# Four unused strips of SBUF that shift where the operands of the matmuls begin

## What is computed

```
def swiglu(h, w_gu, w_down):
    gu = h @ w_gu
    return (jax.nn.silu(gu[..., :D_FF]) * gu[..., D_FF:]) @ w_down       # D_FF = 2816

def first_block(...):                       # x: tokens, z: context
    for i in range(2):                      # two layers
        x = ffn_sublayer(x, ...); z = ffn_sublayer(z, ...)
        # layer 0: short_conv_mixer(x), short_conv_mixer(z); layer 1: window_attention_mixer(hx, hz)
        x = adaln_out(x, yx, ...)
        x = ffn_sublayer(x, ...)            # and z in layer 0
    return x

def second_block(...):                      # x alone
    proj = rms_norm(x, g_mix) @ w_in        # 13 pieces: queries, keys, values, gates
    merged = sigmoid(gate_a) * (nsa_mixer(...) @ w_up_nsa) + sigmoid(gate_b) * (moba_mixer(...) @ w_up_moba)
    x = x + merged @ w_out
    gate, up = jnp.split(rms_norm(x, g_ffn) @ w_ffn_in, 2, axis=-1)
    x = x + (jax.nn.silu(gate) * up) @ w_ffn_out
    return x + sigmoid(rms_norm(x, g_ple) @ w_ple_gate) * (p @ w_ple_proj)
```

## Time and profile before

| | us |
|---|---|
| three timed runs | 2218.05, 2222.94, 2223.88 |
| median | 2222.94 |
| the profiled execution, whole | 2218.97 |
| its span, first to last instruction | 2217.6 |
| mean granted TensorE clock in it | 0.989 of full speed |
| TensorE busy with matmuls | 2121.8 (96%) |
| TensorE busy with weight loads (beside them) | 1914.7 (86%) |
| VectorE busy | 1525.9 (69%) |
| ScalarE busy | 1045.5 (47%) |
| GpSimd busy | 90.1 (4%) |

### The profile page before, as it was taken

The page is one execution under the profiler, slowest core; times in us unless marked ns, Lnnn a source line. Parts: engine busy times, 40 slices in busy tenths (PEclk is TensorE's granted clock), DMA queues, the critical chain, the costliest instruction groups (busy, mean ns, idle before and its releaser), DMA issues. The chain is left out here.

```text
span 2217.6 us, 35178 instructions
## 1 busy us (share of the span) xinstructions
PE 2121.8 (96%) x14546; PEld 1914.7 (86%) x14546; DVE 1525.9 (69%) x2435; ACT 1045.5 (47%) x1675; POOL 90.1 (4%) x67
## 2 busy tenths in 40 slices
PE   6999999999989999999999999997999899999998
PEld 4988889998889888899988889857999887799998
DVE  3665776777675667767566776785767666777665
ACT  5622224663474222257422235675544544665444
POOL 0000000100100000010000001001000101000000
PEclk9999999999999999999999999999999999999999
DMA  7545555455435455544545544502455552245544
GB/s 307 201 166 194 190 181 176 157 183 197 153 134 185 167 200 192 177 162 154 193 163 206 192 166 163 181 23 96 164 217 185 181 200 87 77 157 179 202 172 151
DMA packets 70015, 378.77 MB, mean 171 GB/s; under 512 B 7392, under 2 KB 12384, under 8 KB 42976
## 3 DMA queue, kind: packets, MB, share of 16 engines
q1 hardware_dynamic: 66960, 369.92, 47.5%
q10 hardware_dynamic: 2896, 6.60, 0.8%
HBM read 375.45 MB, written 1.05 MB: 170 GB/s over the span
## 5 line engine op out<-in xcount | busy, mean ns | idle before, releaser
L549 PE MATMUL ps_g<-h,w_hi 128*128 128x256 f32 (+2 forms) x4288 | 985.2, 324 | 25.6 <-DVE h L1044 7.7
L931 DVE TENSOR_TENSOR w_lo<-w_raw,w_hi 128x1024 fp32r<-128x1024 f32 (+2 forms) x614 | 688.1, 1123 | 388.1 <-ACT w_hi L1521 386.7
L1521 ACT ACTIVATE w_hi<-w_raw 128x1024 fp32r<-128x1024 f32 (+2 forms) x614 | 590.0, 967 | 529.6 <-PE ps_g L549 373.1
L549 PEld LDWEIGHTS ps_g<-h,w_hi 128*128 128x128 f32 x4288 | 717.8, 190 | 97.4 <-issue 15.1
L549 PE MATMUL ps_g<-h,w_lo 128*128 128x256 f32 (+2 forms) x2144 | 690.2, 322 | 0.0
L549 PE MATMUL ps_g<-hid,w_hi 128*128 128x256 f32 (+1 forms) x2368 | 498.8, 308 | 13.4 <-DVE y L1113 8.6
L549 PEld LDWEIGHTS ps_g<-h,w_lo 128*128 128x128 f32 x2144 | 406.4, 190 | 32.9
L549 PEld LDWEIGHTS ps_g<-hid,w_hi 128*128 128x128 f32 x2368 | 385.3, 190 | 38.6 <-DVE w_lo L931 9.8
L549 PE MATMUL ps_g<-hid,w_lo 128*128 128x256 f32 (+1 forms) x1184 | 362.1, 306 | 0.0
L549 PE MATMUL ps_g<-b_h,w_hi 128*128 128x256 f32 x1504 | 274.1, 284 | 10.2 <-DVE b_h L1044 7.2
L549 PEld LDWEIGHTS ps_g<-b_h,w_hi 128*128 128x128 f32 x1504 | 231.5, 190 | 18.0 <-issue 17.2
(11 more groups left out here) (274 smaller groups left out, 1588.8 us busy)
## 6 DMA issues: line engine op xcount, KB each, us to landing
w_raw<-in_gu SPq DMA_DIRECT2D x130, 1024.0 KB, 4.8
mod_raw<-in_w_mod SPq DMA_DIRECT2D x128, 512.0 KB, 3.5
w_raw<-in_conv_cu SPq DMA_DIRECT2D x16, 1024.0 KB, 4.8
w_raw<-in_dn00b SPq DMA_DIRECT2D x16, 768.0 KB, 4.2
w_raw<-in_dn01b SPq DMA_DIRECT2D x16, 768.0 KB, 4.2
w_raw<-in_dn10b SPq DMA_DIRECT2D x16, 768.0 KB, 4.2
w_raw<-in_conv_out SPq DMA_DIRECT2D x8, 1024.0 KB, 4.8
w_raw<-in_w_in_a SPq DMA_DIRECT2D x8, 1024.0 KB, 4.9
```

Of the source, the lines that this page charges most:

```text
L549: mm = pe.matmul(at, w[wp][:, k, m * P:(m + 1) * P], acts[ap][:, k, cs], start=(k == 0 and n == 0 and not (one_bank and m)), stop=(k == kc ...
L931: dve.tensor_tensor(w_lo[u % 2][:, cols], w_raw[u % 2][:, cols], w_hi[u % 2][:, cols].bitcast(F32), ALU.subtract).then_inc(lo_made, 1)
L1521: act.activation(w_hi[u % 2][:, cols], w_raw[u % 2][:, cols], ACT.Copy).then_inc(hi_made, 1)
```

## The change

Four tiles that nothing reads or writes are put among the others, and the tile `skip2`, also unused, is made 512 bytes smaller. No instruction is added, taken away or moved, on any engine.

```diff
     b1 = ExitStack()
+    sb("fill0", [P, 32], F32, b1)
     h1 = [sb(f"h{j}", [P, NC, T2], F32R, b1) for j in range(2)]
     wide = sb("wide", [P, 2, 2, S + 2], F32, b1)
     cond_b = sb("cond_b", [P, 2, D], F32, b1)
+    sb("fill1", [P, 120], F32, b1)
     early1 = ExitStack()
...
     b2 = ExitStack()
+    sb("fill2", [P, 16], F32, b2)
     h2 = [sb(f"b2_h{j}", [P, NC, S], F32R, b2) for j in range(2)]
     apart2 = ExitStack()
     qk = sb("qk", [P, 18, S], F32, apart2)
     apart2.close()
     h3 = [sb(f"b2_h3_{j}", [P, NC, S], F32R, b2) for j in range(2)]
-    sb("skip2", [P, 2, S], F32, b2)
+    sb("skip2", [P, 2 * S - P], F32, b2)
     gates = sb("gates", [P, 2 * NC, S], F32, b2)
     v_tok2 = sb("v_tok", [P, 2, 3 * S], F32, b2)
     flat = sb("flat", [P, 2, 16, 32], F32, b2)
     rope2 = sb("rope2", [P, 2, S], F32, b2)
     causal = sb("causal", [P, S + 30], F32, b2)
+    sb("fill3", [P, 112], F32, b2)
```

## The result

| | before | after |
|---|---|---|
| median of 20 timed runs each, us | 2221.39 | 2226.36 |
| lowest to highest, us | 2216.64 to 2224.74 | 2220.65 to 2232.15 |
| span of the profiled execution, us | 2217.6 | 2222.6 |
| mean granted TensorE clock | 0.989 | 0.989 |

The ratio after to before is 1.0025, its 95% interval 1.0016 to 1.0033. The changed kernel is 5 us slower. That is less than the 0.3% that the prediction took as the limit of a measurement, but 20 runs of each tell it from nothing. The forecast was 2169 us with a range up to 2219, so it missed, and in sign.

A forecast was written before the change was run, and what follows sets the result against it. TensorE, busy for 96% of the span, was taken as the bound, by how fast matmuls follow each other. Gains of 30.7 + 7.6 + 4.5 + 4.5 + 3.4 + 3.0 = 53.7 us gave 2169 us, range 2152 to 2219.

The forecast's parts named there:

- Term 1: 512-column products of h and hid: step falls from 228.9 and 233.5 to 220.1 ns, 30.7 us faster.
- Term 4: 256-column products of hid: up to 6.7 ns less each, little where loads bind; 7.9 us faster.
- Term 2: 256-column products of h: high level falls to low, 4.3 ns each, half counted beside norms; 7.6 us faster.
- Term 3: 258-column products of h, 1056 in all: 4.3 ns less each, 4.5 us faster.
- Term 5: b_h moved to 128 past the weights: 3.0 us faster, bounds 7.9 faster and some 7.3 slower.
- Term 6: Other tiles that moved (wide, cond_b, kv_raw, q_raw, qk, gates, v_tok), without long matmuls: counted as nothing.
- only the multiple of 64 counts: hid's products fall to the high level, nothing else changes: 5.3 us faster, 2218 us; chance 0.13.
- nothing does: Steps differ for another reason and addresses are bystanders: no effect, 2223 us; chance 0.08.
- The rival called slower: h at 512 columns goes to 233.5 ns, deciding from 2.2 ns; net 12.5 us slower, 2235 us; chance 0.12.

The follow-up runs named there:

- hid alone: Only hid moved, from 96 to 192 bytes past the weights, against the kernel before: 2214.73 us against 2222.77, ratio 0.9965.
- the parts: Three kernels moving only h, only hid or only b_h against the kernel before: +7.9, -8.0 and +3.7 us, which sum to +3.6 us.

## Why the prediction was wrong

**Term 1, the 512 columns, failed, and with it the sign.** The step that failed is "it is the same loss, in proportion to the columns streamed". It was drawn from two starts, 64 and 96, where the excesses at 512 columns happened to be twice those at 256. From it followed that a start with a low level at 256 has one at 512, of 220.1 ns. There is none: 192 is the best start for 256 columns and among the worst for 512, and 0 is the other way round. Measured +10.6 and 0.0 us where 30.7 us less were forecast. The prediction itself named that carry-over as the step on which more than half of the whole hung, and no row stood behind it: b_hid, the one tile at 192, never streams 512 columns.

**Term 4, hid at 256 columns, was right in mechanism and too small.** 192 takes hid from 120 to 113.3 or 117.8, and the change gained 11.1 us there for 7.9, hid alone 8.0 on the metric. The loads were expected to bind in the down projections; in dn3b they didn't, TensorE waited for nothing and the phase took 32.5 us. dn4b at the same step takes 35.0 and did so before as well, of which 2.4 us are pauses; its chain runs over loads whose start hangs on w_lo, and w_lo there waits behind ScalarE's work for the last norm. I took the one for the other. Where norms run beside the gain was small (dn0bz 42.1 us before and after, dn1bz and dn2bz 0.3 and 0.4 us less): the step came down only in part, and the waits for y grew, in dn0bz from 2.5 to 3.8 us.

**Term 2, h at 256 columns, was nearly nothing** (-0.7 for -7.6). 192 is low more often than 64, but not always. Over all profiles, with stretches of 24 matmuls free of waits and of the lower clock, 647 of 1151 were low at 192 and 52 of 969 at 64. gu1az and gu2az fell by 1.3 and 1.4 us, gu0az stayed at 117.8 in the first profile and was partly low in the second. What they gained was lost again in gu0ax (+1.6) and gu1ax (+1.2); in gu1ax the granted clock was 0.97 where the before had 1.00. Whether that has to do with the change is not shown. The idea of the prediction, that at these two starts it is decided by how things fell after a wait, has the repeated executions for it. That 192 is reliably low has them against it, b_hid too: w_up, on which the prediction built, is low in seven of the ten profiles in which it stands at 192. Nor does b_hid always turn round the level that it takes over. With h alone moved, gu4a was high and dn4a behind it as well:

```profile
L551 PE MATMUL ps_g<-b_hid,w_hi x160: 280/281/281, 2065.8 to 2093.8; 128*128 128x256 f32 x160
```

And conv_cuz, counted as low already, was so by luck: with h at 64 it is low in one profile of six.

**Term 3, 258 columns**, was taken for 256 columns with two more. At 192 they are at 120.0 or 120.8, worse than at 64: +1.5 for -4.5.

**Term 5, b_h at 128**, was bounded by a loss of 7.3 us and taken as a gain of 3.0 because 128 lies between two known starts. It has a level of its own, 118.7 in every execution: a loss of 3.7 (the interval reaches from 0 to 5). Between two rows there was no reason to put the value near their mean.

**Term 6, the tiles that moved along**, at nothing: the parts leave 1.4 us, well within their intervals, so it is neither confirmed nor refuted to better than some 5 us.

**The rivals.** Those in which only the multiple of 64 counts, or nothing does, fall: 0, 64, 128 and 192 all differ. The rule quoted from the Trainium skill ("TensorE: Matmul & The Clock Gate", "Step-by-step: what each phase is for"), that loading the next weights takes no SBUF read bandwidth from a running matmul, doesn't carry to "no distance can matter": with the weights alone moved by 128 bytes the step went from 228.9 to 233.3 ns. That the two reads get into each other's way would fit this, but no run shows where the time goes. The 215.8 ns that the formula of the same page of the Trainium skill gives for 512 columns ("Back-to-back issue gap") was never reached; the best was 226.7. The rival called slower was right for h at 512 columns (11.0 us priced, 10.6 measured), and its mark of 2.2 ns there was passed with 4.4. It went too far in the rest, since hid's gain at 256 columns, priced at 2.0 us, was 11.1. I gave it 0.12, though it alone rested on a row of the right form: hid's 233.5 was the only second start at 512 columns that the trace had.

**Open**: why the table repeats after 256 bytes and has these entries, what in a wait decides between 113.4 and 117.8, and what took 258 columns at 64 to 122.2 once. No experiment changed a wait and nothing else.

## What to carry to other kernels

Where matmuls with a weight load each follow one another without idle time, read the step by form (columns, streamed tile, loaded tile) and write the distance of the two starts beside it before touching anything; carry a level over to another number of columns only if a row of that form shows it. An offset inside a double buffer cost no time here, and 512 bytes a partition for each buffer; it lets each phase have its own distance, which together with the strip ahead of hid was worth 0.95%, whereas one strip ahead of a tile moves all its products at once and gave one form what it took from another. Before a low stretch counts as a property of the code, look at a second execution, and before a longer phase counts as a slower step, look at its granted clock.

## What the runs showed of the hardware

The step in ns of back-to-back float32r matmuls with a weight load each, by distance modulo 256 bytes, from all profiles above, in stretches without waits at a granted clock of 1.00:

| distance | 512 columns | 256 columns | 258 columns |
|---|---|---|---|
| 0 | 226.7 | 120.0 | 120.8 |
| 32 | 233.3 | 116.7 or 117.8 | 120.0 |
| 64 | 228.9 | 113.3 or 117.8 | 118.7 or 119.0, once 122.2 |
| 96 | 233.3 | 120.0 | not run |
| 128 | 233.3 (one phase 232.3) | 118.7 | 120.0 or 122.2 |
| 160 | not run | 117.3 or 118.7 | not run |
| 192 | 233.3 | 113.3 or 117.8 | 120.0 or 120.8 |
| 224 | 233.3 | 118.3 | not run |

Three things of it were unexpected. The step depends on where two tiles stand to each other in SBUF at all, by up to 2.9% at 512 columns and 5.8% at 256. The order of the starts differs with the columns. And at 64 and 192 one program has two levels at 256 columns and falls to either, phase by phase and execution by execution. That made 1.6 of the 6.7 us between the spans 2217.6 and 2224.3 of the same kernel, and as much came from a lower granted clock in the one phase w_up.
